# Scores, diagonal and reads of the old states in 32-column strips at four PSUM row ranges of TensorE

## The reference

```python
def step(S, inp):
    qc, kc, vc, gc = inp
    b = jnp.cumsum(gc, axis=2)
    o_inter = jnp.einsum('bhtk,bhkv->bhtv', qc * jnp.exp(b), S)
    diff = b[:, :, :, None, :] - b[:, :, None, :, :]
    decay = jnp.where(causal, jnp.exp(jnp.where(causal, diff, 0.0)), 0.0)
    scores = jnp.einsum('bhtk,bhsk,bhtsk->bhts', qc, kc, decay)
    o = o_inter + jnp.einsum('bhts,bhsv->bhtv', scores, vc)
    ...
# per layer, on RMS-normed x:
proj = h @ w_in_l                       # 1024 x 9232 columns, split among:
# q, k, v, g, gate rank of GLA (4 heads, dk 128, dv 256)
# q, f, i, g of HGRN2 (8 heads, 128 x 128), two merge gates
# both recurrences, head norms, gates, sum, @ w_out_l, norm,
# then norm, SwiGLU (2 x 2816 columns in, 2816 rows out), norm
```

## Time and profile before

| | before |
|---|---|
| median of 3 runs | 1216.9 us (1214.06 to 1219.04) |
| the profiled execution's own time | 1218.76 us |
| its span | 1217.0 us |
| TensorE matmul busy | 1169.4 us, 96% |
| VectorE, ScalarE, GpSimd busy | 679.9, 480.1, 45.4 us |
| mean granted TensorE clock | 0.979 |
| instruction fetch | 1.06 MB in 65 packets and 0.17 MB in 21 |

### The profile page before, as it was taken

One profiled execution on the slowest core, in us unless ns is written; L12 is line 12 of the kernel. 1 busy time (PEld: TensorE's weight loads), 2 busy tenths in 40 slices (PEclk: granted clock), 3 DMA queues, 4 the chain that ended last, 5 costly groups with the idle time before them and its releaser, 6 DMA issues.

```text
span 1217.0 us, 19467 instructions
## 1 busy us (share of the span) xinstructions
PE 1169.4 (96%) x8188; PEld 1107.3 (91%) x8188; DVE 679.9 (56%) x973; ACT 480.1 (39%) x765; POOL 45.4 (4%) x72
## 2 busy tenths in 40 slices
PE   4999999999999999999999999978999999999998
PEld 4999999799999899999899997768999999988886
DVE  4254442354442455533454544769999999874544
ACT  4432243432244432143522244455444444453532
POOL 5000000100000100000100000000000000000000
PEclk8999998899999899999999999989999999999999
DMA  6421122421122411223421215502333233232222
GB/s 178 126 71 53 53 79 69 139 71 53 53 78 85 142 53 53 69 62 103 130 64 53 67 47 156 164 0 79 95 105 104 80 95 105 87 120 71 87 69 78
DMA packets 138598, 104.84 MB, mean 86 GB/s; under 512 B 3968, under 2 KB 123776, under 8 KB 138512
## 3 DMA queue, kind: packets, MB, share of 16 engines
q1 hardware_dynamic: 133648, 85.78, 25.0%
q0 software_dynamic: 4864, 17.83, 4.8%
HBM read 91.79 MB, written 11.80 MB: 85 GB/s over the span
## 4 chain that ended last, share of the span: by engine, by line
PE 90%; DVE 5%; ACT 2%; DVEq 1%; issue 1%; ACTq 0%; POOL 0%; DMA 0%; POOLq 0%
PE ps L250 39%; PE ps L1636 18%; PE ps L1658 12%; PE ps L912 6%; PE ps L339 4%; PE ps L947 2%; PE ps L955 2%; PE ps L962 1%; PE ps L941 1%; PE ps L931 1%; DVE w_lo_t L240 1%; PE ps L943 1%; PE ps L893 1%; ACT w_hi_t L236 1%; PE ps L924 1%
## 5 line engine op out<-in xcount | busy, mean ns | idle before, releaser
L250 PE MATMUL ps<-x_hi,w_lo_t 128*128 128x288 f32 x1168 | 260.0, 305 | 4.5 <-DVE w_lo_t L240 4.5
L250 PE MATMUL ps<-x_lo,w_hi_t 128*128 128x288 f32 x1168 | 253.0, 299 | 0.0
L250 PE MATMUL ps<-x_hi,w_hi_t 128*128 128x288 f32 x1168 | 252.9, 298 | 0.0
L236 ACT ACTIVATE w_hi_t<-w_raw_t 128x1024 fp32r<-128x1024 f32 x73 | 77.2, 1058 | 389.8 <-PE ps L250 378.4
L240 DVE TENSOR_TENSOR w_lo_t<-w_raw_t,w_hi_t 128x1024 fp32r<-128x1024 f32 x75 | 91.7, 1222 | 212.4 <-ACT w_hi_t L236 212.4
L250 PEld LDWEIGHTS ps<-x_hi,w_lo_t 128*128 128x128 f32 x1168 | 191.4, 193 | 8.2 <-DVE w_lo_t L240 4.6
L250 PEld LDWEIGHTS ps<-x_lo,w_hi_t 128*128 128x128 f32 x1168 | 191.7, 192 | 0.0
L250 PEld LDWEIGHTS ps<-x_hi,w_hi_t 128*128 128x128 f32 x1168 | 190.8, 191 | 0.0
L720 DVE TENSOR_TENSOR Q<-Q,B 128x768 f32<-128x768 f32 (+1 forms) x24 | 23.8, 992 | 114.7 <-PE ps L912 76.6
L1636 PE MATMUL ps<-x_hi,w_lo_t 128*128 128x288 f32 x264 | 78.7, 298 | 5.6 <-issue 4.2
L1636 PE MATMUL ps<-x_lo,w_hi_t 128*128 128x288 f32 x264 | 78.4, 297 | 0.0
(11 more groups left out here) (278 smaller groups left out, 2175.3 us busy)
## 6 DMA issues: line engine op xcount, KB each, us to landing
w_raw_t<-in_w_in_dram SPq DMA_DIRECT2D x73, 512.0 KB, 3.8
merged<-in_w_ffn_in_dram SPq DMA_DIRECT2D x22, 512.0 KB, 5.3
w_raw_t<-in_w_ffn_in_dram SPq DMA_DIRECT2D x22, 512.0 KB, 5.0
w_raw_t<-in_w_ffn_out_dram SPq DMA_DIRECT2D x22, 512.0 KB, 3.8
h_t<-in_x_prompt_dram SPq DMA_DIRECT2D x8, 512.0 KB, 6.8
h_t<-in_state_gla_dram POOLq DMA_DIRECT2D x4, 1024.0 KB, 6.2
h_t<-in_state_hgrn_dram POOLq DMA_DIRECT2D x8, 512.0 KB, 8.0
out_dram<-h_t POOLq DMA_DIRECT2D x4, 1024.0 KB, 5.3
```

The costliest lines, as they stand in the source:

```text
L236: nc.scalar.activation(w_hi_t[:, u % NSPL, 0:nk, :], w_raw_t[:, u % NRAW, 0:nk, :], ACT.Copy).then_inc(w_hi, 1)
L250: m = nc.tensor.matmul(out[:, q, :], w[:, u % NSPL, k, :], x(k, q), start=first and i == 0, stop=last and i == len(todo) - 1)
```

## The change

The products of the diagonal, of the levels and of the old sample states are cut along the stationary columns. Where one matmul had 128 stationary columns and wrote PSUM partitions 0 to 127, four matmuls now have 32 stationary columns each and write partitions 0 to 31, 32 to 63, 64 to 95 and 96 to 127. For the diagonal and the levels, a strip of 32 keys needs only its own 32 tokens of queries, so the moving side is cut too: 32 columns instead of 128 in `diag`, 16 instead of 64 in a level. Level 5 (L = 32) takes two products of 32 by 32 for each of its twelve (chunk, head) pairs, at partitions 0 and 64, and level 6 (L = 64) one product of 64 by 64. The samples' diagonal and levels take two strips. For the old states the moving side stays at 8 columns.

The blocks off the diagonal strips are no longer written in PSUM, so VectorE copies the diagonal by predicate, with the identity as the mask, and Am and As are zeroed once by GpSimd at the start. Levels 5 and 6 are now plain copies on VectorE.

```diff
+STRIP = 32
...
+        for t in (Am, As):
+            nc.gpsimd.memset(t[:], 0.0).then_inc(consts, 1)
+            n += 1
...
+            if L >= 32:
+                for t in range(0, C, 2 * L):
+                    ins = dve.tensor_copy(Am[t:t + L, :, t + L:t + 2 * L],
+                                          s[t:t + L, 0:3 * NC * C // 2].rearrange("p (h r) -> p h r", r=C // 2)[:, :, t // 2:t // 2 + L])
+                freed(ins, j, f"level{i}")
+                return
...
+            one = ident[:, :].bitcast(I32).rearrange("p (o t) -> p o t", o=1)
             if i < 2:
-                ins = dve.tensor_tensor(Am[:, 6 * i:6 * i + 6, :], s[:, 0:6 * C].rearrange("p (h t) -> p h t", t=C),
-                                        ident[:, :].rearrange("p (o t) -> p o t", o=1).broadcast_to([P, 6, C]), ALU.mult)
+                ins = dve.copy_predicated(Am[:, 6 * i:6 * i + 6, :], one.broadcast_to([P, 6, C]),
+                                          s[:, 0:6 * C].rearrange("p (h t) -> p h t", t=C))
...
-                for a in range(6 if i < 2 else 0):
+                for a in range(6 if i < 2 else 3):
                     c, h = divmod(6 * i + a, 3)
-                    m = nc.tensor.matmul(s[:, a * C:(a + 1) * C], K[:, h, c * C:(c + 1) * C], Q[:, h, c * C:(c + 1) * C],
-                                         start=True, stop=True)
...
+                    width = C if i < 2 else TS
+                    for t in range(0, width, STRIP):
+                        cols = slice(c * C + t, c * C + t + STRIP)
+                        m = nc.tensor.matmul(s[t:t + STRIP, a * width + t:a * width + t + STRIP], K[:, h, cols], Q[:, h, cols], start=True, stop=True)
...
-                    m = nc.tensor.matmul(s[:, a * C // 2:(a + 1) * C // 2], K[:, h, c * C:(c + 1) * C], second(Q[:, h, c * C:(c + 1) * C], L),
-                                         start=True, stop=True)
+                    o = a * C // 2
+                    if L >= 32:
+                        for t in range(0, C, 2 * L):
+                            m = nc.tensor.matmul(s[t:t + L, o + t // 2:o + t // 2 + L], K[:, h, c * C + t:c * C + t + L],
+                                                 Q[:, h, c * C + t + L:c * C + t + 2 * L], start=True, stop=True)
+                    else:
+                        for t in range(0, C, STRIP):
+                            m = nc.tensor.matmul(s[t:t + STRIP, o + t // 2:o + (t + STRIP) // 2], K[:, h, c * C + t:c * C + t + STRIP],
+                                                 second(Q[:, h, c * C + t:c * C + t + STRIP], L), start=True, stop=True)
...
-                    nc.tensor.matmul(s[:, TP + b * SL:TP + (b + 1) * SL], st, Q[:, h, TP + b * SL:TP + (b + 1) * SL],
-                                     start=(b == 0), stop=False, skip_group_check=True)
+                    for v in range(0, P, STRIP):
+                        nc.tensor.matmul(s[v:v + STRIP, TP + b * SL:TP + (b + 1) * SL], st[:, v:v + STRIP], Q[:, h, TP + b * SL:TP + (b + 1) * SL],
+                                         start=(b == 0), stop=False, skip_group_check=True)
```

More of the change, by code:

```diff
@@ L747, in diagonal @@
             s = step(j, f"diag{i}")
+            one = ident[:, :].bitcast(I32).rearrange("p (o t) -> p o t", o=1)
             if i < 2:
-                ins = dve.tensor_tensor(Am[:, 6 * i:6 * i + 6, :], s[:, 0:6 * C].rearrange("p (h t) -> p h t", t=C),
-                                        ident[:, :].rearrange("p (o t) -> p o t", o=1).broadcast_to([P, 6, C]), ALU.mult)
-            else:
-                ins = dve.tensor_tensor(As[:, :, :], s[0:TS, 0:3 * TS].rearrange("p (h t) -> p h t", t=TS),
-                                        ident[0:TS, 0:TS].rearrange("p (o t) -> p o t", o=1).broadcast_to([TS, 3, TS]), ALU.mult)
+                ins = dve.copy_predicated(Am[:, 6 * i:6 * i + 6, :], one.broadcast_to([P, 6, C]),
+                                          s[:, 0:6 * C].rearrange("p (h t) -> p h t", t=C))
+            else:
+                ins = dve.copy_predicated(As[:, :, :], one[0:TS, :, 0:TS].broadcast_to([TS, 3, TS]),
+                                          s[0:TS, 0:3 * TS].rearrange("p (h t) -> p h t", t=TS))
             freed(ins, j, f"diag{i}")
@@ L897, in do_step @@
                     pe.wait_ge(qk_in, j + 1)
-                for a in range(6 if i < 2 else 0):
+                for a in range(6 if i < 2 else 3):
                     c, h = divmod(6 * i + a, 3)
-                    m = nc.tensor.matmul(s[:, a * C:(a + 1) * C], K[:, h, c * C:(c + 1) * C], Q[:, h, c * C:(c + 1) * C],
-                                         start=True, stop=True)
-                if i == 2:
-                    for h in range(3):
-                        m = nc.tensor.matmul(s[0:TS, h * TS:(h + 1) * TS], K[:, h, TP:T], Q[:, h, TP:T],
-                                             start=True, stop=True)
+                    width = C if i < 2 else TS
+                    for t in range(0, width, STRIP):
+                        cols = slice(c * C + t, c * C + t + STRIP)
+                        m = nc.tensor.matmul(s[t:t + STRIP, a * width + t:a * width + t + STRIP], K[:, h, cols], Q[:, h, cols], start=True, stop=True)
             elif name[:5] == "level":
@@ L916, in do_step @@
                         o = 3 * NC * C // 2 + h * TS // 2
-                        m = nc.tensor.matmul(s[0:TS, o:o + TS // 2], K[:, h, TP:T], second(Q[:, h, TP:T], L), start=True, stop=True)
+                        for t in range(0, TS, STRIP):
+                            m = nc.tensor.matmul(s[t:t + STRIP, o + t // 2:o + (t + STRIP) // 2], K[:, h, TP + t:TP + t + STRIP],
+                                                 second(Q[:, h, TP + t:TP + t + STRIP], L), start=True, stop=True)
             elif name[:2] == "kt":
@@ L1688, in build @@
     keep.close()
-CONSTS = 4 + 1 + 2 * NL + 2
+CONSTS = 6 + 1 + 2 * NL + 2
 SETUP = 1
```

## The result

The changed kernel takes 1147.55 us, median of 4 runs (1146.36 to 1148.94), against 1217.45 us for the kernel before in the same rounds (1214.06 to 1219.04). The ratio is 0.943, 95% interval 0.9407 to 0.9453.

What follows compares the result with a forecast made beforehand. TensorE was taken to bound the kernel, except at the diagonal. Savings of 12.3 us a group, 49 us for four, less 9 us for the clock, came off 1218.8 us, stated as 1180 us, range 1160 to 1240 us.

Steps and rivals of the forecast that it cites:

- What bounds the kernel: TensorE, busy 96% of the span: time its queue saves comes off the span, except at the diagonal.
- The price at one place: A pair with 32 stationary columns costs 32.1 ns on TensorE without overlap, from a line through 64 and 128 columns.
- The overlap: Strips at different row places on TensorE work partly at once: 12.3 ns a pair at four places, 19.9 at two.
- Ways in and out: On TensorE, a stretch with narrower tiles costs 0.24 us on the way in and out together.
- The clock: Half-clock stretches at diagonals and levels 0 to 2: eight new, less two that go, 9 us lost.
- The rules weighed: Skill rules for TensorE strips: three column tiles at 2.38 times serial speed; matmul starts never closer than about 25 ns.
- Serial loads: Rival: strip loads are served one after another, 25.4 ns a pair whatever the place, about 1222 us; chance 0.13.
- no overlap: Rival: strips at different places do not overlap at all, 32.1 ns a pair, about 1259 us; chance 0.12.
- the clock rival: Rival: overlap as forecast, but the clock falls at every level and diagonal, about 1218 us; chance 0.08.
- given-back time: Rival: something behind TensorE becomes late and part of the saved time is lost, about 1198 us; chance 0.07.
- The sum: Whole kernel: 49 us saved less 9 us for the clock, 40 us off the profiled execution's 1218.8 us.

Runs made afterwards that it cites:

- e1_one_place: The changed kernel with all strips of levels 0 to 4 at one PSUM place and zero masks, leaving those levels out of the output; 1199.7 us.
- e5_levels_only: The changed kernel with full-width matmuls again for the diagonal and the reads of old states, only the levels in strips; 1173.1 us (0.9655).
- e6_states_only: The kernel before the change with only the reads of the old states in strips; 1195.4 us (0.9837).

## Why the prediction was off

- *What bounds the kernel.* Right. TensorE's time came off the span, and the one exception, the diagonal, is where it was put: a wait of 2.40 us against 2.3 forecast. Where the clock stayed up its gain was 0.1 us, as read in the second group. In the first group the distance to level 0 grew from 10.47 to 11.88 us, because the clock fell behind the hole.
- *The price at one place.* Right. 32.1 ns, read as a line through 64 and 128 columns, against 32 in `e1_one_place`.
- *The overlap.* This step failed, and it is the term that made the forecast too small: "I take 0.62 × 0.62 × 32.1 = 12.3 ns at four places and 0.62 × 32.1 = 19.9 ns at two". The runs gave 8.5 and 16 ns, the lower bound of the range. The mechanism was right and the factor mis-sized, and the trace held the better one. I divided the whole 1.09 us of L962 by its 16 pairs, with the ways in and out in it, though I had priced these ways myself two paragraphs on. Inside a run of the kernel before the same line reads:

```profile
394.34 0.49 PE L962 MATMUL ps<-v_t,B 32*128 32x128 f32 x5
```

  These are the pairs under way in a window of 0.02 us at 394.56, the oldest from 394.34. The last two begin at 394.68. Pairs start there two at a time every 0.11 us, so 394.68 is six starts later: 56 ns a pair, half of the 110 of one place, not 0.62. A half taken twice of 32.1 is 8.0 ns. The term came out at 16.0 us a group instead of 12.3, 15 us in all.
- *Ways in and out.* 0.24 us forecast for levels 3 to 6. Level 4 saves 1.54 us from slot to slot; 2.60 − 96 × 8.5 ns would be 1.78. So they cost 0.24, right.
- *The clock.* This step failed as well: "eight new stretches, three at the diagonals and five at levels 0 to 2, less two that go, 6 × 1.5 = 9 us". No stretch came at the levels, two came at the diagonals, and all of those behind the `o` steps went, 17 us or five stretches, where the forecast had two; what was forecast as 9 us lost became some 5 us gained. `e5_levels_only` and `e6_states_only` show that these falls came with the full-width reads with 8 moving columns and went with them.
- *The rules weighed.* The Trainium skill's tile speed-ups ("TensorE: Matmul & The Clock Gate", Part 3: Packing small matmuls) pointed to the right side. The Trainium skill's floor of about 25 ns between starts ("Back-to-back issue gap") does not hold across places, since 26 pairs start in 0.22 us, and at one place the 32 ns a pair lie above it, so it can't be seen there.
- *The rivals.* Serial loads and no overlap are refuted by the three place counts, the clock rival by 1.00 in 90 to 160 us, and given-back time by the slots: level 4 itself got 1.67 us shorter and its slot 1.54, which leaves 0.13 us for the way in. Two sums among the rivals are a little off. With the terms given, no overlap loses 3.3 us a group (13 in all, not 14), and the change would have lost from a pair price of 28 ns, not 27; neither moves a chance.
- *The sum.* 40 us forecast off the profiled execution, plus 15 for the overlap, plus 16 for the clock (9 not lost, 5 gained) and the rest, gives the 71 of the spans.

## What to carry to other kernels

Where a float32 matmul is bound by its weight load and its output needs only a block diagonal, cut the stationary side into strips at different PSUM row places, and change the place with every matmul or every second one: the price falls with the number of places, down to the larger of load and stream of one place over their count. Read the price of an overlapped run between two starts inside it, never as its length over its count, and then look for the buffers that the freed PSUM columns make unnecessary; here that gave another 11 us by the ratios.

## What the hardware showed that was not expected

- The overlap between four column places is whole: 32, 16 and 8.5 ns a pair at one, two and four places, with four loads and, at 64 moving columns, four streams at once (14.4 ns a pair).
- Up to four pairs in a row at one place cost little (1.06 against 0.93 us a level); six, eight, twelve and twenty-four cost 1.65, 2.04, 2.44 and 2.85.
- Levels of 3.1 us at a single place of the array kept the granted clock at 1.00, while 1.8 us of full-width matmuls with 8 moving columns, among other steps, stood before each fall to 0.50 behind an `o` step (190 us before, 191 in `e5_levels_only`). So a small part of the array in use did not by itself bring the clock down here. Whether it is the width or the length of the reads no run shows.
